# Fused block kernel: the Toeplitz matrix behind the c row and nine modulation tiles on GpSimd's DMA queue

## The chip, the cores and the metric

One core of one Trainium2 chip runs the kernel. The metric is the time of one execution in microseconds (us). The engines are TensorE (PE, with its weight loads as PEld), VectorE (DVE), ScalarE (ACT), GpSimd (POOL) and SyncE (SP). SP, ACT and POOL issue DMAs: SP on queue q1, ACT on q10, POOL on q0. Data moves between HBM, SBUF (the on-chip memory that the engines read) and PSUM (where TensorE writes, as `bank0` to `bank7`).

## The reference

One layer in float32, for 256 tokens of width 1024, cut to what matters here:

```
mod = silu(c) @ w_ada + b_ada                    # six rows of 1024: sh1 sc1 ga1 sh2 sc2 ga2
h   = rms_norm(x) * g_mix * (1 + sc1) + sh1      # and the same for 256 context tokens
proj = h @ w_in                                  # -> u_a (512), z_b (2 x 512), gate logits (2 x 1024)
y   = u_a * d + forward and backward S5 state-space scans over u_a, started from the context's state
y_a = gelu(y) * sigmoid(gelu(y) @ w_glu + b_glu)
y_b = gated spatial mixing of z_b (128-token chunks)
x   = x + ga1 * ((g_a * (y_a @ w_proj_a) + g_b * (y_b @ w_proj_b)) @ w_out)
h2  = rms_norm(x) * g_ffn * (1 + sc2) + sh2
x   = x + ga2 * (silu(gate) * val) @ w_down      # gate, val = 3x3 depthwise conv of h2 @ w_up
out = rms_norm(x) * g_final
```

## The kernel before

Everything runs once, in an order written out by hand for each engine; the engines meet through semaphores. A semaphore that a DMA raises goes up by 16.

**The weights** come in units of 1 MB (128 partitions x 2048 float32). SP loads 21 units into a ring of four slots (L312 to L334): unit u is issued when unit u - 4 has been multiplied (`s_unit`). Units 8 to 15 are the gate weights (`gate_unit(0)` to `gate_unit(7)`, L566), unit 16 is the GLU weight, 17 to 20 the projection weights. So the end of gate 1 releases unit 13 (gate 5), the end of gate 2 unit 14 (gate 6), the end of gate 3 unit 15 (gate 7), the end of gate 4 unit 16. Four units of `w_out` go to their own place (`s_wo`), and six units of `w_up` are issued at L335 to L337, once all 24 modulation sums are done (`s_mt_used` is MT = 24).

**The S5 branch.** The inputs of the scans are computed by chunks of 8 tokens (`chunk_inputs`, L553). A Toeplitz matrix holds what the tokens of a chunk do to each other. It is computed by TensorE, copied by ACT and stored to `k_scratch` in HBM (`s_k_out`), and read back from there by eight DMAs of POOL, shifted by one lag each, into `m_toep` (L371 to L374, 256 KB each in rows of 512 bytes; `s_m`). TensorE multiplies with it at L629 to L637, after gate 5; then come gate 6, the product with the scan's carries (L641 to L651), gate 7, eight transposes (L656 to L660) and three projections of y_b. DVE adds the skip term u * d (L1430 to L1435, called the skip below), ACT applies gelu (L920), TensorE the GLU product (L684 to L693), ACT the sigmoid, DVE the product y_a (L1440 to L1442), TensorE the remaining projections (L697 to L704). For each of the eight output tiles DVE merges the two branches (L1449 to L1457). The out stage (L706 to L731 on TensorE) multiplies with `w_out` by seven Strassen products, for which DVE forms sums (L1463 to L1476).

**The modulation rows** ga1, sh2 and sc2 are not matrix products: for each of MT = 24 tiles of 128 outputs, POOL loads a tile of w_ada (512 KB, `mod_tile`), and DVE multiplies it with the row silu(c) and sums over it (`modulation_sums`, L1415 to L1422). The row c is loaded by POOL (`c_bc`, L377, 512 KB) and put through silu by ACT (L905). MTS = 9 buffers hold the tiles; seven of them and `c_bc` lie where the scan's input weights were, which are free when the last chunk input is in PSUM (`s_e_ps` is 8), and the last two where the gating parameters were (`s_sgu_ps` is 2). Tile t >= 9 is issued when sum t - 9 is done. The first eight sums give ga1 (L1426), the other sixteen sh2 and sc2 (L1479). POOL's queue goes on with the reload of x (L385), the row ga1 (L389) and the row g_final (L391).

**Order on POOL**: gating parameters, eight Toeplitz DMAs, wait for all of them to land, c row, 24 tiles, x, ga1, g_final.
**Order on DVE from the scan on**: scan, y_b, sums 0 to 11, ga1, skip, sums 12 to 17, y_a, sums 18 and 19, then one sum behind each of the first four merges, the sums for the out stage, the modulation result (L1479), the updates of x.

Of the kernel before, what the change touches and what calls it, by code (L numbers as in the profile page):

```python
# [30 lines left out]
G, H, N = 32, 16, 64  # L31
# [3 lines left out]
T = 8  # L35
# [18 lines left out]
MT = 3 * KD  # L54
MTS = 9
# [24 lines left out]
def build(nc, x_t, x_tok, ctx_t, pk, s5raw, early_w, ring_w, out_w, up_w, ln, sgu_w, sgu_b, mod_w, c_row, g_row, out):  # L80
    with ExitStack() as ctx:
# [3 lines left out]
        def sem(name):  # L85
            return ctx.enter_context(nc.semaphore(name))
# [12 lines left out]
        m_toep = m_region.rearrange("p (g m) -> p g m", g=G)  # L99
# [101 lines left out]
        def par(name):  # L201
            a, b = _PK[name]
            return pk_sb[:, a:b]
# [9 lines left out]
        k_dram = nc.dram_tensor("k_scratch", [KS, P, LAGS * H], F32)  # L213
# [31 lines left out]
        s_k_ps, s_k, s_k_out, s_m = sem("k_in_psum"), sem("k_evacuated"), sem("k_stored"), sem("m_loaded")  # L245
# [29 lines left out]
        s_mt_used = sem("mod_tile_summed")  # L275
# [76 lines left out]
        @block.gpsimd  # L352
        def _(pool):
            pool.memset(ones[:, :], 1.0).then_inc(s_const, 1)
            pool.memset(c_pad, 0.0).then_inc(s_cpad, 1)
            pool.memset(ident[:, :], 0.0).then_inc(s_pool, 1)
            pool.wait_ge(s_pool, 1)
            pool.affine_select(out=ident[:, :], in_=ident[:, :], compare_op=ALU.not_equal, fill=1.0, base=0,
                               pattern=[[-1, P]], channel_multiplier=1).then_inc(s_const, 1)
            pool.wait_ge(s_ctx, 16)  # L360
            for k in CTX_SQUARES[2]:
                pool.tensor_tensor(h_all[:, k, 0:TOK], ctx_sb[:, k, :], ctx_sb[:, k, :], ALU.mult).then_inc(s_sqc[2], 1)
            pool.wait_ge(s_ada_ps, 2)
            pool.wait_ge(s_wsrc, 1)
            pool.memset(b_pad, 0.0).then_inc(s_pad, 1)
            pool.wait_ge(s_unit, U_V)
            pool.dma_start(sgu_b_sb[0:64, :, :], sgu_b[0:1].partition_broadcast(64)).then_inc(s_ln, 16)
            pool.dma_start(sgu_b_sb[64:128, :, :], sgu_b[1:2].partition_broadcast(64)).then_inc(s_ln, 16)
            pool.dma_start(ln_sb, ln.partition_broadcast(P)).then_inc(s_ln, 16)
            pool.dma_start(sgu_w_sb, sgu_w).then_inc(s_ln, 16)  # L370
            pool.wait_ge(s_k_out, 16)  # L371
            for tau in range(T):
                pool.dma_start(m_toep[tau * H:(tau + 1) * H, :, :],  # L373
                               k_dram[:, :, (T - 1 - tau) * H:(2 * T - 1 - tau) * H].rearrange("m (g h) n -> h (m g) n", h=H)).then_inc(s_m, 16)  # L374
            pool.wait_ge(s_e_ps, 8)
            pool.wait_ge(s_m, 16 * T)
            pool.dma_start(c_bc, c_row.partition_broadcast(P)).then_inc(s_crow, 16)  # L377
            for t in range(MT):
                if t == S5_TILES:
                    pool.wait_ge(s_sgu_ps, 2)  # L380
                if t >= MTS:
                    pool.wait_ge(s_mt_used, t - MTS + 1)
                pool.dma_start(mod_tile[t % MTS], mod_w[t].rearrange("p (k n) -> p k n", k=4)).then_inc(s_mt[t % MTS], 16)  # L383
            pool.wait_ge(s_y8_ps, 2)
            pool.dma_start(x1_tok.rearrange("p h f n -> p (h f n)"), x_tok).then_inc(s_xr, 16)  # L385
            pool.wait_ge(s_ga1_out, 16)
            pool.wait_ge(s_ya, KS)
            pool.wait_ge(s_unit, U_GLU + 1)
            pool.dma_start(ga1_bc.rearrange("p f n -> p (f n)"), ga1_dram[:].partition_broadcast(P)).then_inc(s_ga1_row, 16)  # L389
            pool.wait_ge(s_unit, U_PROJ + 3)  # L390
            pool.dma_start(g_bc.rearrange("p f n -> p (f n)"), g_row.partition_broadcast(P)).then_inc(s_grow, 16)  # L391
            pool.sem_inc(s_act, 2)
            with pool.Fori(0, KF // 2) as i:
                for b in range(2):
                    pool.wait_ge(s_silu, i * 2 + (b + 1))
                    pool.tensor_tensor(ffn_act[:, bass.ds(i * 2 + b, 1), :].rearrange("p a t -> p (a t)"), silu_sb[:, b, :],  # L396
                                       conv[:, b, TOK:2 * TOK], ALU.mult).then_inc(s_act, 1)
# [641 lines left out]
        def _(dve):  # L1039
# [7 lines left out]
            def settle():  # L1047

                dve.wait_ge(s_dve, count[0])

            def tt(o, a, b, op):
                mark(dve.tensor_tensor(o, a, b, op))  # L1052
# [298 lines left out]
            for j in range(1, BLK):  # L1351
                h = blocks[:, j - 1]
# [51 lines left out]
            for j in range(4):  # L1404
# [3 lines left out]
                t = merge_tmp[:, j % 2, :]  # L1408
# [6 lines left out]
            def modulation_sums(t0, t1):  # L1415

                for t in range(t0, t1):
                    dve.wait_ge(s_mt[t % MTS], 16 * (t // MTS + 1))
                    if t == 0:
                        dve.wait_ge(s_cbc, 1)  # L1420
                    dve.scalar_tensor_tensor(out=mod_tile[t % MTS], in0=mod_tile[t % MTS], scalar=1.0, in1=c_bc4, op0=ALU.mult, op1=ALU.mult,  # L1421
                                             accum_out=mod_sum[:, t:t + 1]).then_inc(s_mt_used, 1)  # L1422

            modulation_sums(0, 12)
            dve.wait_ge(s_mt_used, 12)
            dve.tensor_tensor(mod2[:, 0:KD], mod_sum[:, 0:KD], par("b_ada")[:, 2 * KD:3 * KD], ALU.add).then_inc(s_ga1, 1)  # L1426

# [6 lines left out]
                                             scalar=par("s5_d")[:, m:m + 1], in1=y_ps[:, m], op0=ALU.mult, op1=ALU.add).then_inc(s_y, 1)  # L1435

            modulation_sums(12, 18)

            for m in range(KS):  # L1440
                dve.wait_ge(s_glu, m + 1)
                dve.tensor_tensor(y_a[:, m, :], y_gelu[:, m, :], glu_gate[:, m, :], ALU.mult).then_inc(s_ya, 1)  # L1442

            modulation_sums(18, 20)

            wo11, wo12, wo21, wo22 = w_out[:, :, 0, 0, :], w_out[:, :, 0, 1, :], w_out[:, :, 1, 0, :], w_out[:, :, 1, 1, :]
# [1 line left out]
            for m in range(KD):  # L1449
                dve.wait_ge(*((s_unit, U_PROJ + m // 2 + 1) if m % 2 else (s_pr_ps, m // 2 + 1)))  # L1450
                src = bank[PROJ_BANK[m % 4]]
                t = merge_tmp[:, 0, :], merge_tmp[:, 1, :]
                tt(t[0], src[:, 0:TOK], gates[:, m, :], ALU.mult)
                tt(t[1], src[:, TOK:2 * TOK], gates[:, KD + m, :], ALU.mult)
                settle()
                dve.tensor_tensor(merged[:, m, :], t[0], t[1], ALU.add).then_inc(s_mg, 1)
                dve.wait_ge(s_mg, m + 1)  # L1457
                if m < MT - 20:
                    modulation_sums(20 + m, 21 + m)
                elif m == 6:  # L1460
                    for i in range(KD // 2):
                        dve.wait_ge(s_wo[i], 16)
                    dve.tensor_tensor(out_t1, wo12, wo11, ALU.subtract).then_inc(s_to, 1)  # L1463
# [10 lines left out]
            dve.tensor_tensor(out_s[2], m12, out_s[1], ALU.subtract).then_inc(s_so, 1)  # L1474
            dve.tensor_tensor(m21, m11, m21, ALU.subtract).then_inc(s_so, 1)
            dve.tensor_tensor(wo12, wo22, wo12, ALU.subtract).then_inc(s_to, 1)  # L1476

            dve.wait_ge(s_mt_used, MT)
            dve.tensor_tensor(mod2[:, KD:MT], mod_sum[:, KD:MT], par("b_ada")[:, 3 * KD:5 * KD], ALU.add).then_inc(s_mod2, 1)  # L1479
# [293 lines left out]
```

## Time and profile before

| | |
|---|---|
| three runs | 465.65, 466.66, 468.84 us; median 466.66 |
| the profiled execution | 465.06 us, of which the span is 463.2 |
| DMA | 98.47 MB, mean 213 GB/s |
| queue q1 (SP) | 72.34 MB, 44.8% of 16 engines' span |
| queue q0 (POOL) | 18.61 MB, 12.9% |
| TensorE's mean granted clock | 0.999 |

The span is what lies between the first and the last instruction of the profiled execution. Busy time says how full an engine was, not what it held up: an engine that is idle while another one has work costs nothing. A bracket behind a row of a timeline gives the idle time in front of it, and what ended it. DMA shares are of the 16 DMA engines' time.

### The profile page before, as it was taken

The page shows a single profiled execution, that of the slowest core. Times are in us where ns is not written, and L with a number is a line of the kernel's source. Part 1 is how long each engine was busy: PE and PEld are TensorE (multiplying, and loading weights), DVE is VectorE, ACT ScalarE, POOL GpSimd, SP SyncE. Part 2 cuts the span into 40 slices and gives each one's busy share as a digit, 9 for nine tenths or more (in the row PEclk, how much of TensorE's full clock was granted, in tenths as well). Part 3 has the DMA queues.
Part 4 walks back from the last instruction along what each step waited for, and adds up shares of the span by engine and source line. Part 5 has one row for each costly group of instructions (what it writes and reads, how often), then busy time and mean ns, then how long its engine had stood idle before and what let it go on. Part 6 is the DMA issues. An engine that isn't in the chain of part 4 may idle for free.

```text
span 463.2 us, 7678 instructions
## 1 busy us (share of the span) xinstructions
PE 447.6 (97%) x2637; PEld 345.0 (74%) x2637; DVE 401.2 (87%) x818; ACT 116.5 (25%) x216; POOL 45.3 (10%) x73
## 2 busy tenths in 40 slices
PE   8999999989999998999999999999999999999994
PEld 5677857888888886785478888888888887444453
DVE  3599999999999867969836999999999999899744
ACT  5423355135104023201152222122122122200002
POOL 2001100002104222000000111011011011000000
PEclk9999999999999999999999999999999999999999
DMA  8994499943999999989069554554554354400002
GB/s 300 418 420 162 130 347 87 299 161 72 109 219 411 419 392 399 416 342 398 3 253 405 206 190 148 209 226 162 200 201 150 147 181 70 158 0 0 1 0 91
DMA packets 24604, 98.47 MB, mean 213 GB/s; under 512 B 7608, under 2 KB 9280, under 8 KB 16128
## 3 DMA queue, kind: packets, MB, share of 16 engines
q1 hardware_dynamic: 14592, 72.34, 44.8%
q0 software_dynamic: 5056, 18.61, 12.9%
q10 hardware_dynamic: 4928, 7.14, 4.2%
q8 instruction: 18, 0.29, 0.3%
q14 instruction: 10, 0.08, 0.1%
HBM read 95.49 MB, written 2.60 MB: 212 GB/s over the span
## 4 chain that ended last, share of the span: by engine, by line
PE 59%; DVE 20%; DMA 16%; POOL 2%; ACT 1%; issue 1%; DVEq 0%; SPq 0%; ACTq 0%; POOLq 0%
PE bank L756 33%; PE bank L767 14%; DVE s_region L1052 11%; DMA h_all<-mod_w 9%; PE bank L711 5%; DMA s_region<-k_scratch 5%; PE bank L667 5%; DVE s_region L1171 2%; DMA ctx_region<-ctx_t 2%; DVE s_region L1309 1%; DVE h_all L1225 1%; POOL s_region L373 1%; PE bank L482 1%; POOL s_region L383 1%; DMA k_scratch<-s_region 1%
## 5 line engine op out<-in xcount | busy, mean ns | idle before, releaser
L756 PE MATMUL bank<-h_all,s_region 128*128 128x256 f32 x704 | 152.3, 379 | 0.2 <-ACT h_all L966 0.2
L756 PEld LDWEIGHTS bank<-h_all,s_region 128*128 128x128 f32 x704 | 133.2, 190 | 19.1 <-ACT h_all L966 0.6
L1571 DVE SCALAR_TENSOR_TENSOR ctx_region<-ctx_region,pk_sb 128x189 f32<-128x189 f32 (+2 forms) x352 | 130.2, 443 | 0.3 <-DVE ctx_region L1571 0.2
L573 PE MATMUL bank<-h_all,ring_region 128*128 128x256 f32 x256 | 56.2, 380 | 0.3 <-DVE s_region L1340 0.3
L573 PEld LDWEIGHTS bank<-h_all,ring_region 128*128 128x128 f32 x256 | 48.4, 190 | 7.4 <-DVE s_region L1340 0.5
L767 PE MATMUL bank<-s_region,ring_region 128*128 128x512 f32 (+1 forms) x132 | 47.8, 522 | 0.0
L767 PEld LDWEIGHTS bank<-s_region,ring_region 128*128 128x128 f32 x132 | 25.0, 190 | 22.5 <-issue 20.3
L984 ACT ACTIVATE ctx_region<-bank 128x512 f32<-128x512 f32 x22 | 13.1, 597 | 113.3 <-PE bank L756 60.1
L1052 DVE TENSOR_TENSOR s_region<-s_region,power 128x2048 f32<-128x2048 f32 (+1 forms) x16 | 38.1, 2420 | 0.2
L396 POOL TENSOR_TENSOR ring_region<-gates,ctx_region 128x256 f32 x22 | 17.2, 784 | 178.2 <-ACT gates L992 178.2
L482 PE MATMUL bank<-h_all,ring_region 128*128 128x256 f32 x128 | 31.1, 388 | 0.2 <-ACT h_all L829 0.2
L1421 DVE SCALAR_TENSOR_TENSOR s_region<-s_region 128x1024 f32<-128x1024 f32 x20 | 24.1, 1223 | 7.8 <-DMA s_region<-mod_w 7.6
L667 PE MATMUL bank<-z_region,ring_region 128*128 128x256 f32 x128 | 28.2, 380 | 1.1 <-DVE z_region L1442 1.1
L482 PEld LDWEIGHTS bank<-h_all,ring_region 128*128 128x128 f32 x128 | 23.3, 190 | 5.9 <-ACT h_all L829 2.5
L667 PEld LDWEIGHTS bank<-z_region,ring_region 128*128 128x128 f32 x128 | 24.2, 190 | 4.7 <-DVE z_region L1442 1.5
L1560 DVE TENSOR_SCALAR ctx_region<-ctx_region,pk_sb 128x256 f32<-128x256 f32 x22 | 11.5, 521 | 11.6 <-ACT ctx_region L984 10.9
L871 ACT ACTIVATE gates<-bank,pk_sb 128x256 f32<-128x256 f32 x16 | 6.7, 470 | 39.6 <-PE bank L573 39.6
L533 PE MATMUL bank<-ring_region,h_all 128*128 128x512 f32 x32 | 16.4, 593 | 0.0
L1017 ACT ACTIVATE z_region<-s_region 128x512 f32<-128x512 f32 (+1 forms) x4 | 2.3, 573 | 50.3 <-DVE s_region L1637 31.6
L829 ACT ACTIVATE h_all<-h_all,mod,scale 128x256 f32<-128x256 f32 x16 | 8.8, 594 | 23.7 <-DVE scale L1233 21.6
L521 PEld LDWEIGHTS bank<-ident,s_region 128*128 128x128 f32 x64 | 7.9, 141 | 8.8 <-issue 7.9
L711 PE MATMUL bank<-s_region,h_all 128*128 128x512 f32 (+1 forms) x40 | 14.2, 507 | 0.0
(242 smaller groups left out, 529.5 us busy)
## 6 DMA issues: line engine op xcount, KB each, us to landing
s_region<-up_w SPq DMA_DIRECT2D x33, 1024.0 KB, 4.9
ring_region<-ring_w SPq DMA_DIRECT2D x20, 1024.0 KB, 9.0
s_region<-mod_w POOLq DMA_DIRECT2D x20, 512.0 KB, 15.4
s_region<-early_w SPq DMA_DIRECT2D x4, 1024.0 KB, 21.8
s_region<-out_w SPq DMA_DIRECT2D x4, 1024.0 KB, 12.7
gates<-mod_w ACTq DMA_DIRECT2D x8, 512.0 KB, 5.4
gates<-early_w SPq DMA_DIRECT2D x2, 1024.0 KB, 10.8
s_region<-k_scratch POOLq DMA_DIRECT2D x8, 256.0 KB, 12.4
```

Of the source, the lines that this page charges most:

```text
L396: pool.tensor_tensor(ffn_act[:, bass.ds(i * 2 + b, 1), :].rearrange("p a t -> p (a t)"), silu_sb[:, b, :], conv[:, b, TOK:2 * TOK], ALU.mu ...
L482: mx = pe.matmul(bank[m][:, cols], ring[:, U_INU + k // 4, ((k % 4) * KS + m) * P:((k % 4) * KS + m + 1) * P], h_all[:, k, cols], start=(k ...
L533: mx = pe.matmul(bank[6 + c][:, :], h_x[:, k, c * P:(c + 1) * P], ring[:, u % RING, kk * 512:(kk + 1) * 512], start=(k == 0), stop=(k == K ...
L573: mx = pe.matmul(bank[5 - j % 2][:, mm * TOK:(mm + 1) * TOK], ring[:, u % RING, (mm * KD + k) * P:(mm * KD + k + 1) * P], h_x[:, k, :], st ...
L667: mx = pe.matmul(bank[PROJ_BANK[m % 4]][:, (1 - half) * TOK:(2 - half) * TOK], ring[:, u % RING, t * P:(t + 1) * P], src[:, k, :], start=( ...
L711: mx = pe.matmul(bank[OUT_BANK[n]][:, cols], lhs(i), rhs(i)[:, cols], start=(i == 0 and n not in (3, 6, 7)), stop=(i == KD // 2 - 1), skip ...
L756: mx = pe.matmul(bank[s % 3][:, half * TOK:(half + 1) * TOK], up_ring[:, s, (half * KD + k) * P:(half * KD + k + 1) * P], h2[:, k, :], sta ...
L767: mx = pe.matmul(bank[PRODUCT_BANK[n]][:, cols], lhs(i), rhs(i)[:, cols], start=(i == 0), stop=(i == PAIRS_D - 1))
L984: act.activation(up_sb[:, j % 2, :], bank[(j % USLOTS) % 3][:, :], ACT.Copy).then_inc(s_upsb, 1)
L1052: mark(dve.tensor_tensor(o, a, b, op))
L1421: dve.scalar_tensor_tensor(out=mod_tile[t % MTS], in0=mod_tile[t % MTS], scalar=1.0, in1=c_bc4, op0=ALU.mult, op1=ALU.mult, accum_out=mod_ ...
L1571: dve.scalar_tensor_tensor(out=o, in0=a, scalar=cw[:, tile[half], (dy + 1) * 3 + dx + 1], in1=o, op0=ALU.mult, op1=ALU.add).then_inc(s_con ...
```

## The change

On POOL the wait for the last chunk input, the c row and the first nine tiles (0 to 8) now stand ahead of the Toeplitz matrix, whose eight DMAs are issued when the loop reaches t = MTS = 9; the wait for their landing on POOL is gone (TensorE's own wait at L629 stays). On DVE nine sums, not twelve, stand ahead of the skip, five between the skip and y_a (9 to 13), three behind y_a (14 to 16), one behind each of the first six merges (17 to 22), and the last one (23) behind the sums of the out stage. The number of DMAs, sums and matmuls stays the same.

```diff
-            pool.wait_ge(s_k_out, 16)
-            for tau in range(T):
-                pool.dma_start(m_toep[tau * H:(tau + 1) * H, :, :],
-                               k_dram[:, :, (T - 1 - tau) * H:(2 * T - 1 - tau) * H].rearrange("m (g h) n -> h (m g) n", h=H)).then_inc(s_m, 16)
             pool.wait_ge(s_e_ps, 8)
-            pool.wait_ge(s_m, 16 * T)
             pool.dma_start(c_bc, c_row.partition_broadcast(P)).then_inc(s_crow, 16)
             for t in range(MT):
                 if t == S5_TILES:
                     pool.wait_ge(s_sgu_ps, 2)
+                if t == MTS:
+                    pool.wait_ge(s_k_out, 16)
+                    for tau in range(T):
+                        pool.dma_start(m_toep[tau * H:(tau + 1) * H, :, :],
+                                       k_dram[:, :, (T - 1 - tau) * H:(2 * T - 1 - tau) * H].rearrange("m (g h) n -> h (m g) n", h=H)).then_inc(s_m, 16)
                 if t >= MTS:
                     pool.wait_ge(s_mt_used, t - MTS + 1)
...
-            modulation_sums(0, 12)
-            dve.wait_ge(s_mt_used, 12)
+            modulation_sums(0, 9)
+            dve.wait_ge(s_mt_used, 9)
...
-            modulation_sums(12, 18)
+            modulation_sums(9, 14)
...
-            modulation_sums(18, 20)
+            modulation_sums(14, 17)
...
-                if m < MT - 20:
-                    modulation_sums(20 + m, 21 + m)
+                if m < 6:
+                    modulation_sums(17 + m, 18 + m)
...
             dve.tensor_tensor(wo12, wo22, wo12, ALU.subtract).then_inc(s_to, 1)
+            modulation_sums(23, MT)
```

## Rows read from the trace of the kernel before

**Rows 1.** The page, part 1: busy us, share of the span, instructions.
```profile
PE 447.6 (97%) x2637; PEld 345.0 (74%) x2637; DVE 401.2 (87%) x818; ACT 116.5 (25%) x216; POOL 45.3 (10%) x73
```

**Rows 2.** Timeline of PE: start us, us, engine, line, operation, count [idle before it <-what ended it].
```profile
108.25 2.08 PE L562 MATMUL bank<-ctx_region,s_region 128*64 128x64 f32 x64
...
147.07 1.95 PE L635 MATMUL bank<-s_region,ctx_region 128*32 128x128 f32 x64
...
170.93 1.04 PE L658 MATMUL bank<-ident,ctx_region 128*128 128x128 f32 x8
...
176.98 0.27 PE L682 MATMUL bank<-ident,mod 128*8 128x128 f32 x1
179.51 7.14 PE L688 MATMUL bank<-u_x,ring_region 128*128 128x256 f32 x32 [2.26 <-ACT u_x L920]
186.49 1.89 PE L667 MATMUL bank<-z_region,ring_region 128*128 128x256 f32 x8
189.47 20.99 PE L667 MATMUL bank<-z_region,ring_region 128*128 128x256 f32 x96 [1.09 <-DVE z_region L1442]
...
238.50 21.71 PE L756 MATMUL bank<-h_all,s_region 128*128 128x256 f32 x99 [0.15 <-ACT h_all L966]
```

**Rows 3.** Timeline of DVE.
```profile
155.28 1.22 DVE L1421 SCALAR_TENSOR_TENSOR s_region<-s_region 128x1024 f32<-128x1024 f32 x1
...
175.10 2.15 DVE L1434 SCALAR_TENSOR_TENSOR ctx_region<-u_x,pk_sb,bank 128x128 f32<-128x128 f32 x8
...
187.99 1.43 DVE L1442 TENSOR_TENSOR z_region<-u_x,ctx_region 128x256 f32<-128x256 f32 x4
...
207.12 0.76 DVE L1052 TENSOR_TENSOR merge_tmp<-bank,gates 128x256 f32<-128x256 f32 x2 [2.24 <-PE bank L667]
...
221.53 0.69 DVE L1052 TENSOR_TENSOR gates<-ctx_region,u_x 128x512 f32<-128x512 f32 x1 [1.60 <-ACT ctx_region L936]
```

**Rows 4.** Timeline of ACT: gelu, and the last two sigmoids of the GLU.
```profile
177.29 2.08 ACT L920 ACTIVATE u_x<-ctx_region 128x1024 f32<-128x1024 f32 x1 [3.81 <-DVE ctx_region L1434]
...
186.69 0.84 ACT L929 ACTIVATE ctx_region<-bank,pk_sb 128x256 f32<-128x256 f32 x2 [2.62 <-PE bank L688]
```

**Rows 5.** Timeline of POOL: the issues.
```profile
112.73 5.01 POOL L373 DMA_DIRECT2D s_region<-k_scratch  x8 [54.19 <-DMA k_scratch<-s_region]
...
139.26 3.69 POOL L383 DMA_DIRECT2D s_region<-mod_w  x7
142.91 1.53 POOL L383 DMA_DIRECT2D h_all<-mod_w  x2
```

**Rows 6.** Issues of L373 to landing: least, median, most.
```profile
DMA to landing us min/median/max: 5.5/12.4/21.0
```

**Rows 7.** Windows: us, busy of PE, PEld, DVE, ACT, POOL; clock, DMA share, GB/s.
```profile
120.00:125.00 5.00, 5.00 (x25) 4.41 (x24) 4.86 (x8) 0.39 (x2) 0.00 (x0) 1.00 1.04 108
...
150.00:155.00 5.00, 5.00 (x25) 4.41 (x24) 4.80 (x13) 0.00 (x0) 0.00 (x0) 1.00 1.03 420
```

**Rows 8.** DMA queues, 112.7 to 138.1 us: packets, MB, share of 16 engines.
```profile
q0 software_dynamic: 640, 2.10, 68.5%
q1 hardware_dynamic: 212, 1.61, 28.6%
```

**Rows 9.** DMA, 119.4 to 126.4 us: the only data queue, and the issue of unit 13.
```profile
q0 software_dynamic: 232, 0.76, 104.4%
...
ring_region<-ring_w SPq DMA_DIRECT2D x1, 1024.0 KB, 18.2
```

**Rows 10.** Timelines of PE, at the kernel's start and mid-kernel: the same filler matmuls.
```profile
1.00 5.12 PE L408 MATMUL bank<-ones 128*128 128x256 f32 x14 [1.00 <-POOL ones L354]
...
236.01 1.46 PE L408 MATMUL bank<-ones 128*128 128x256 f32 x6
```

**Rows 11.** The six first issues of up weights on SP, and the page's median landing.
```profile
201.58 3.19 SPq L337 DMA_DIRECT2D s_region<-up_w  x6
...
s_region<-up_w SPq DMA_DIRECT2D x33, 1024.0 KB, 4.9
```

## The prediction

> **What bounds the kernel now.** I read the page's shares first, then TensorE's timeline between 108 and 240 us, then the waits of DVE and ACT at each place where TensorE stood, and last the DMA queues. TensorE is busy for 97% of the span [rows 1], so a change that leaves its work alone can only give back its waits. In the stretch that the change touches there are two: 2.26 us before the GLU product, ended by ACT's gelu, and 1.09 us before the projections of y_a, ended by DVE [rows 2]. Behind both stands DVE's order. The skip starts at 175.10 [rows 3] though TensorE's transposes were done at 170.93 + 1.04 = 171.97 [rows 2]; DVE was still at sums, which waited for tiles. And y_a starts at 187.99 [rows 3] though its last sigmoids end at 186.69 + 0.84 = 187.53 [rows 4], because DVE sat in a sum. The third thing to see is a margin: the Toeplitz product starts at 147.07 without a wait [rows 2], and the last of the eight matrix DMAs lands at 117.1 + 21.0 = 138.1 [rows 5, 6]. That is 9.0 us of slack, and it is what the change spends.
>
> **What it gives back.** Sums 0 to 8 need only tiles that now come early. DVE starts them at 155.28 as before [rows 3]; nine at 1.15 us each (start to start) end by 165.7. The skip then starts when the transposes allow, about 171.6, and lasts 2.15: done by 173.9. Gelu (2.08) ends by about 176.1, ahead of TensorE, which is free for the GLU at 176.98 + 0.27 = 177.25. The wait of 2.26 is gone. Sums 9 to 13 follow the skip, 5 x 1.15 = 5.8 us, done by 179.7; the first sigmoid is not due before half the GLU, 177.25 + 3.6 = 180.8. So y_a can follow each sigmoid; the last is done 0.4 us after the sigmoids' end, inside the projection that TensorE has left (its 1.89 us reach to 0.85 us past them [rows 2, 4]). The 1.09 is gone as well. Gain: **3.35 us**. Nothing else follows on TensorE: it is next late for nothing in this part.
>
> **What the other sums cost: nothing, under these covers.** Behind y_a stand three sums where there were two, +1.15; with no wait ahead of them the merges start about 0.8 us later against TensorE than before. Merges 4 and 5 get a sum each, 2.3 us, against DVE's 2.24 us idle before merge 6 and about 1 us before merge 5 (the former in [rows 3]). Merge 6 comes out on time. Without this cover up to 1 us would go to the out stage. Sum 23 (1.2 us) stands before DVE's 1.60 us wait for ACT's copy [rows 3]; 0.4 us remains, and at worst 1.2 is lost. The six up weights wait for sum 23, so SP issues them not at 201.58 [rows 11] but some 20 us later, near 221 in the old clock. A unit lands in 4.9 us in the median [rows 11] on idle queues, and the first is needed at 238.50 [rows 2]: 10 us to spare. POOL's x, ga1 and g_final move behind tile 23, whose issue now waits for y_a; that is some 4 us for x and nothing for ga1, which waited for y_a already. DVE asks for x and ga1 at 221.5.
>
> **What the matrix costs.** Each term is a shift of 138.1, the old landing.
> - POOL starts on its queue when the last chunk input is done, 108.25 + 2.08 = 110.33 [rows 2], not when the matrix is stored, 112.73 [rows 5]: -2.4.
> - Ahead of the matrix go ten transfers of 512 KB, 5.24 MB. Such data flows at about 0.41 MB per us when the queues are full (420 GB/s in 150 to 155 [rows 7]): +12.7. POOL's issues (ten in about 5.8 us [rows 5]) end near 116.1, long before; its issue speed doesn't decide.
> - Unit 13, issued at 119.4, now falls among the tiles instead of into the matrix: 1.05 MB, +2.5. Gate 5 needs it at 140, so it is in time.
> - That gives 151.0 with as much of SP's traffic beside the matrix as before. In the old run SP's packets held back while the matrix ran: unit 13 was issued at 119.4, and until 126.4 only q0 moved data; it landed 18.2 us after its issue [rows 9]. Between 112.7 and 138.1 q1 got 1.61 MB, 28.6% of the engines' time, and the matrix 68.5% [rows 8]. In the new run unit 14 is issued (126.4) just as the matrix starts (about 127), 15 at 133.3 and 16 at 140.3. All three are there earlier relative to the matrix, so I count one more unit: +2.5.
>
> Landing **153.5**, wait of TensorE 153.5 - 147.1 = **6.4 us**. The bounds: at best no SP packet gets beside the matrix, 151.0 less 28.6% of 25.4 us = 143.8, no wait. At worst units 14 to 16 alternate with it in full: 3.15 MB at 7.3/1.61 us per MB is 14.3 us, against the 7.3 already counted: 158, a wait of 11. I take 6.4 since it is nearest to how rows 8 and 9 split the time. The matrix is costly for its size: 108 GB/s with the engines fully busy, against 420 [rows 7].
>
> A page makes a rule of the sharing. The Trainium skill, "DMA: Bandwidth & Descriptors", section on queues, rings and completion order, says that each DMA engine takes turns between its queues packet by packet. By that rule unit 14 would alternate from its issue, and the landing would be at the upper end, near 158. Rows 9 speak against it for the first 7 us after an issue, and rows 8 for it after that.
>
> Everything behind the Toeplitz product on TensorE moves by the wait. DVE's sums 0 to 8 don't, and the carries are ready by 155, so no second wait is added; the 3.35 stays a gain. **Sum: 6.4 - 3.35 = +3.1 us.** Against the profiled 465.06 that is 468.2; that execution lies 1.6 below the median of the three runs, 466.66, to which I add the same: **469.8 us**.
>
> **The rivals.**
> 1. *The matrix comes in time* (faster). Place: the Toeplitz product. If SP's units keep behind the matrix as unit 13 did in rows 9, it lands by 147.1 and only the gain is left: 466.66 - 3.35 = 463.3. It decides at a landing of 150.4: below that the kernel is faster. For it: rows 9. Against it: the second half of rows 8.
> 2. *The wait also costs TensorE its clock* (slower still). At the start, after an idle stretch, fourteen filler matmuls took 5.12 us; six took 1.46 mid-kernel [rows 10]. At the latter pace fourteen take 3.2, so a start from rest costs 1.9. The longest wait inside the touched stretch is 2.26 us, at a granted clock of 1.00. A wait of 6 us is outside what the trace shows. Time: 469.8 + 1.9 = 471.7. The Trainium skill, "TensorE: Matmul & The Clock Gate", warns that an idle gap in the middle of a kernel puts the array back to 1.2 GHz; by it this rival is the rule whenever the wait comes. No row here shows such a gap.
> 3. *Gate 5 waits instead.* If unit 13 is held behind tiles and matrix together, it lands near 147 instead of 128, gate 5 stands some 7 us from 140, and the Toeplitz product no longer waits: 466.66 + 7 - 3.35 = 470.3. Against it: unit 16, issued at 140.3 among tiles, did not suffer so.
> 4. *The two cancel*: landing near 150.4, no difference. The order on DVE then works and shows nothing.
>
> **How the numbers follow.** Forecast 0.40; rival 2, 0.27; rival 1, 0.15; rival 4, 0.10; rival 3, 0.08. About 1%, 4.7 us, is what a measurement can tell from no change. The gain is capped at 3.35, so faster by over 1% needs something unseen: 0.04. Slower by over 1% needs a wait of 8 us, or 6.1 with the clock's cost: a fifth of the forecast, most of rival 2, half of rival 3, together 0.34. The rest, 0.62, is within 1%. The range leaves out the lower edge of rival 1 and the last tenth above: 464.0 to 475.0.
>
> **What would show it.** In TensorE's timeline: a DMA wait in front of L635 (forecast 6.4 us; none in rival 1), or in front of gate 5 (rival 3). No wait on gelu before L688, none on DVE before the last L667 group. In the queues: the first tiles at about 112, the matrix between 127 and 153 at a little over 100 GB/s. Gate 6 behind the wait at a granted clock below 1.00 would be rival 2. What would make me wrong: a matrix that moves faster once no other issue interrupts it, or DMA engines that serve q0 strictly first.

## The result: 13 us slower, and the profile after

The changed kernel takes 479.65 us in the median of five runs (479.14 to 484.71); the kernel before 466.66 (465.65 to 468.84, five runs). The ratio is 1.031, with an interval of 1.028 to 1.035. The forecast was 469.8 in a range of 464.0 to 475.0: the direction was right, the size was a quarter of the real one. The profiled execution took 481.89 us, 16.8 more than that of before, at a mean granted clock of 0.972. The first row below is the page's part 1, the second the granted clock in 40 equal slices of the span.

```profile
PE 453.3 (94%) x2637; PEld 350.0 (73%) x2637; DVE 400.2 (83%) x818; ACT 116.6 (24%) x216; POOL 45.2 (9%) x73
...
PEclk9999999999997597999999999999999999999998
```

TensorE's share fell from 97% to 94% for the same 2637 matmuls, and the clock, which was at 9 in all forty slices before, has two dips, at 144 to 168 us and at 180 to 192 (the 8 in the last slice lies behind the last matmul). TensorE's timeline shows where; compare [rows 2].

```profile
161.08 3.64 PE L635 MATMUL bank<-s_region,ctx_region 128*32 128x128 f32 x64 [13.84 <-DMA s_region<-k_scratch]
164.65 8.07 PE L573 MATMUL bank<-h_all,ring_region 128*128 128x256 f32 x32
172.65 3.95 PE L648 MATMUL bank<-s_region,x_region 64*32 64x128 f32 x147
177.63 3.84 PE L648 MATMUL bank<-s_region,x_region 64*32 64x128 f32 x109 [1.04 <-issue]
181.40 9.91 PE L573 MATMUL bank<-h_all,ring_region 128*128 128x256 f32 x32
...
197.31 7.07 PE L688 MATMUL bank<-u_x,ring_region 128*128 128x256 f32 x32
204.22 22.61 PE L667 MATMUL bank<-z_region,ring_region 128*128 128x256 f32 x104
...
254.86 7.47 PE L756 MATMUL bank<-h_all,s_region 128*128 128x256 f32 x33 [0.15 <-ACT h_all L966]
```

The Toeplitz product waits 13.84 us for the matrix, where it had not waited. The GLU (L688) and the projections of y_a (joined to the ones before them, L667 x104) come without the brackets of 2.26 and 1.09 us. The first up product starts at 254.86 against 238.50: +16.4 of the 16.8. The parts, counted from start to start: the Toeplitz product starts 14.0 later, of which 13.8 are the wait; 1.7 because it takes 3.64 us and not 1.95; 0.9 for gate 6 (8.07 against 7.17); 0.9 in the second part of the carry product and the gap before it; 2.7 for gate 7 (9.91 against 7.17); less 3.9 between the transposes and the first up product (254.86 - 191.15 = 63.7, against 238.50 - 170.93 = 67.6). Of these 3.9 the two brackets make 3.35. The windows show the clock that goes with the long ones (columns as in [rows 7]).

```profile
150.00:155.00 5.00, 0.00 (x0) 0.00 (x0) 4.79 (x13) 0.00 (x0) 0.00 (x0) 0.50 1.01 215
155.00:160.00 5.00, 0.00 (x0) 0.00 (x0) 4.97 (x10) 0.00 (x0) 1.64 (x3) 0.50 0.99 298
160.00:165.00 5.00, 3.92 (x65) 3.57 (x66) 5.00 (x9) 0.00 (x0) 2.40 (x5) 0.50 0.94 338
...
180.00:185.00 5.00, 5.00 (x41) 3.87 (x31) 0.00 (x0) 1.08 (x2) 0.00 (x0) 0.51 0.02 7
```

0.50 is the lower level, 1.2 GHz. The clock fell while TensorE stood at the wait. At 180 it fell again; there TensorE had not waited for data, but it had just come through small matmuls with a gap of 1.04 us in them.

POOL's issues, and their landing (compare [rows 5, 6]):

```profile
110.46 0.55 POOL L372 DMA_DIRECT2D s_region<-c_row  x1 [51.86 <-PE bank L562]
...
116.15 5.01 POOL L379 DMA_DIRECT2D s_region<-k_scratch  x8
```
```profile
DMA to landing us min/median/max: 17.9/28.5/40.4
```

The last matrix DMA is issued at 120.5 and lands 40.4 us later, at 160.9. The DMA queues tell why. First from 128.5 to 132 us, then from 132 to 158 (columns as in [rows 8]):

```profile
q0 software_dynamic: 174, 0.59, 109.9%
```
```profile
q1 hardware_dynamic: 546, 4.06, 73.8%
q0 software_dynamic: 515, 1.66, 27.4%
```

DVE started the skip as soon as the transposes were done, and its last sum fitted in front of ACT's copy with 0.34 us left (forecast 0.4):

```profile
191.86 2.15 DVE L1434 SCALAR_TENSOR_TENSOR ctx_region<-u_x,pk_sb,bank 128x128 f32<-128x128 f32 x8 [26.10 <-PE bank L658]
...
237.90 0.69 DVE L1052 TENSOR_TENSOR gates<-ctx_region,u_x 128x512 f32<-128x512 f32 x1 [0.34 <-ACT ctx_region L936]
```

### The profile page after: what moved, and what is told of

Read it like the earlier page. It is cut to its first block, busy times and chain, and to the rows that moved or that the text cites. A ratio compares the mean times of both kernels' runs of the same rounds, so it can differ in the third digit from the quotient of the medians.

```text
span 479.9 us, 7677 instructions
## 1 busy us (share of the span) xinstructions
PE 453.3 (94%) x2637; PEld 350.0 (73%) x2637; DVE 400.2 (83%) x818; ACT 116.6 (24%) x216; POOL 45.2 (9%) x73
## 4 chain that ended last, share of the span: by engine, by line
PE 80%; DMA 14%; POOL 2%; issue 1%; SPq 1%; DVE 1%; ACT 0%; DVEq 0%; ACTq 0%
PE bank L756 32%; PE bank L767 12%; DMA s_region<-k_scratch 8%; PE bank L667 6%; PE bank L573 5%; PE bank L482 5%; PE bank L711 5%; DMA s_region<-early_w 4%; PE bank L548 3%; PE bank L533 3%; PE bank L562 2%; DMA s_region<-up_w 2%; PE bank L648 2%; PE bank L521 2%; PE bank L688 1%; PE bank L448 1%
## 5 line engine op out<-in xcount | busy, mean ns | idle before, releaser
L573 PE MATMUL bank<-h_all,ring_region 128*128 128x256 f32 x256 | 59.8, 397 | 0.5 <-DVE s_region L1340 0.5
L573 PEld LDWEIGHTS bank<-h_all,ring_region 128*128 128x128 f32 x256 | 51.0, 201 | 9.0 <-DVE s_region L1340 0.8
L482 PE MATMUL bank<-h_all,ring_region 128*128 128x256 f32 x128 | 31.1, 388 | 0.0
L667 PE MATMUL bank<-z_region,ring_region 128*128 128x256 f32 x128 | 28.0, 379 | 0.0
L482 PEld LDWEIGHTS bank<-h_all,ring_region 128*128 128x128 f32 x128 | 23.3, 190 | 5.7 <-ACT h_all L829 2.3
L667 PEld LDWEIGHTS bank<-z_region,ring_region 128*128 128x128 f32 x128 | 24.2, 190 | 3.3
L1434 DVE SCALAR_TENSOR_TENSOR ctx_region<-u_x,pk_sb,bank 128x128 f32<-128x128 f32 x8 | 2.2, 343 | 26.1 <-PE bank L658 26.1
L383 POOL DMA_DIRECT2D s_region<-mod_w x20 | 10.6, 533 | 77.0 <-DVE s_region L1421 77.0
L635 PE MATMUL bank<-s_region,ctx_region 128*32 128x128 f32 x64 | 3.6, 420 | 13.8 <-DMA s_region<-k_scratch 13.8
L533 PE MATMUL bank<-ring_region,h_all 128*128 128x512 f32 x32 | 16.4, 593 | 0.0
```

The costliest lines, as they stand in the source:

```text
L482: mx = pe.matmul(bank[m][:, cols], ring[:, U_INU + k // 4, ((k % 4) * KS + m) * P:((k % 4) * KS + m + 1) * P], h_all[:, k, cols], start=(k ...
L533: mx = pe.matmul(bank[6 + c][:, :], h_x[:, k, c * P:(c + 1) * P], ring[:, u % RING, kk * 512:(kk + 1) * 512], start=(k == 0), stop=(k == K ...
L573: mx = pe.matmul(bank[5 - j % 2][:, mm * TOK:(mm + 1) * TOK], ring[:, u % RING, (mm * KD + k) * P:(mm * KD + k + 1) * P], h_x[:, k, :], st ...
L667: mx = pe.matmul(bank[PROJ_BANK[m % 4]][:, (1 - half) * TOK:(2 - half) * TOK], ring[:, u % RING, t * P:(t + 1) * P], src[:, k, :], start=( ...
```

## The experiments

Theory: the landing of the matrix sets the time, and it is late because SP's ring units alternate with it packet by packet; the rest of the loss is TensorE's clock; the order on DVE is a gain of its own. Rivals: bytes ahead and the matrix's own slowness; costs of the order on DVE; another cause of the long matmuls. Ratios are to the kernel before on the same chip.

### The two halves of the change

**Only the order on DVE.** POOL's part of the diff taken back.

> The queue order of POOL is that of the kernel before (matrix first, wait for its landing, then c row and tiles); only DVE's order of the sums is that of the changed kernel. Theory (the matrix behind the tiles costs everything, the order of the sums gives 3.35 us): no DMA wait before the Toeplitz product, no gelu wait before the GLU product, none before the projections of y_a; about 463.3 us against 466.7, a ratio of 0.993. Rival (the new order of the sums costs something too, in the merges or the out stage): 466 or more.

461.98 us (ten runs, 461.58 to 465.61), ratio 0.994, interval 0.990 to 0.997. TensorE's timeline:

```profile
147.30 1.96 PE L635 MATMUL bank<-s_region,ctx_region 128*32 128x128 f32 x64
...
177.10 7.07 PE L688 MATMUL bank<-u_x,ring_region 128*128 128x256 f32 x32
184.01 22.61 PE L667 MATMUL bank<-z_region,ring_region 128*128 128x256 f32 x104
...
234.65 27.54 PE L756 MATMUL bank<-h_all,s_region 128*128 128x256 f32 x126 [0.15 <-ACT h_all L966]
```

No bracket is left before L688 and L667. From the Toeplitz product to the first up product it takes 87.4 us, against 91.4 [rows 2]: 4.1 less, the 3.35 of the two waits and small overlaps. Of it 3.9 lie behind the transposes, as in the changed kernel. The gain is real and does not need the early tiles.

**Only the order on POOL.** DVE's part taken back.

> POOL's queue order is that of the changed kernel, DVE's order of the sums that of the kernel before. Theory: the same wait of about 14 us before the Toeplitz product and the same clock losses behind it, and since DVE has the wait to catch up in, the gelu wait is gone as well: 478 to 481 us, a ratio of 1.025 to 1.032. Rival (a good part of the loss comes from the order on DVE): below 474.

479.44 us, ratio 1.032 (1.026 to 1.038). There is no wait before the GLU, and one of 14.91 us before the Toeplitz product:

```profile
162.00 3.64 PE L635 MATMUL bank<-s_region,ctx_region 128*32 128x128 f32 x64 [14.91 <-DMA s_region<-k_scratch]
165.57 7.47 PE L573 MATMUL bank<-h_all,ring_region 128*128 128x256 f32 x32
...
180.81 7.17 PE L573 MATMUL bank<-h_all,ring_region 128*128 128x256 f32 x32
```

In this execution the clock fell at the wait alone; gate 7 took its 7.17 us. All of the loss is on POOL's queue, and there the sums' order no longer matters, since DVE catches up during the wait.

### What makes the matrix late

**SP holds the ring from unit 14 on.**

```diff
-            with sp.Fori(2, full) as i: ...
+            for u in range(2 * RING, UNITS):
+                sp.wait_ge(s_unit, u - RING + 1)
+                if u == 14:
+                    sp.wait_ge(s_m, 16 * T)
                 ...
```

> The changed kernel, but SP does not issue unit 14 (gate 6) and those behind it until the matrix has landed (SP's loop is written out; nothing else differs). Theory of the alternation (from about 132 us on every packet of the matrix waits for an 8 KB packet of the ring, units 14 to 17): alone the matrix needs some 18 to 20 us, so it lands near 147 to 149 instead of 160.9; unit 14 then lands 5 us later, and gate 6 stands for it until 152 to 154. Both waits together 4 to 6 us, less the 3.35: 467 to 470 us. Rival (the matrix is late because of the 5 MB ahead and its own slowness, whatever the ring does): it lands at 157 or later, and 478 or more.

The timeline of TensorE, the landing of the matrix, and q0 from 130 to 144 us, where no other data queue moved:

```profile
147.30 1.95 PE L632 MATMUL bank<-s_region,ctx_region 128*32 128x128 f32 x64
151.88 8.86 PE L570 MATMUL bank<-h_all,ring_region 128*128 128x256 f32 x32 [2.63 <-DMA ring_region<-ring_w]
```
```profile
DMA to landing us min/median/max: 17.8/22.7/26.7
```
```profile
q0 software_dynamic: 543, 1.77, 102.9%
```

The same tiles are ahead, and the matrix lands at 120.4 + 26.7 = 147.1: TensorE does not wait for it. Alone it moved 39 records (0.126 MB) per us, next to the ring 20 (0.064 MB). The rival is refuted: 13.8 of the 13.8 us between the two landings are the four units. The time was still 473.8 us (ratio 1.020, 1.014 to 1.027), more than the 467 to 470 that I had expected: gate 6 stood 2.63 us for unit 14, and in that execution the clock fell behind that wait and again in the carry product (gate 6 took 8.86 us, gate 7 9.42).

**SP holds the ring from unit 16 on.** The same edit with `u == 16`.

> The changed kernel, but SP holds unit 16 and those behind it until the matrix has landed, so that units 14 and 15 alternate with it and 16 and 17 don't (all four held: landing 147.1; none held: 160.9). Theory of the alternation (each unit beside the matrix costs it the same): about half of the difference, landing 153 to 155, a wait of 6 to 8 us; 471 to 476 us, according to the clock. Rival (only the unit that is in flight at the end of the matrix counts, or only the first one): landing within 2 us of 147 or of 161.

```profile
155.83 3.64 PE L632 MATMUL bank<-s_region,ctx_region 128*32 128x128 f32 x64 [8.52 <-DMA s_region<-k_scratch]
```

476.26 us (ratio 1.020, 1.017 to 1.023), the matrix in at 155.7. Of SP's units beside it none, two and four give 147.1, 155.7 and 160.9: 4.3 us each for the first two, 2.6 each for the others, the last of which was issued only at about 147.3. Each is one profiled execution, and with all four beside it the landing varied from 160.9 to 163.2, so the split is rough.

**The matrix late, with no tile near it.** POOL as before, DVE as changed, and

```diff
             pool.wait_ge(s_k_out, 16)
+            pool.wait_ge(s_unit, U_GATE + 3)
```

> The version with only DVE's order changed, but POOL waits with the matrix until gate 2 is done (126.4 us); c row and tiles stay behind its landing, so no tile is near it. Theory (the tiles matter only because they move the matrix beside units 14 to 17): data from 127.7, packets of the ring beside it from about 131, landing 159 to 162, a wait of 12 to 14 us, as in the changed kernel; 476 to 483 us. Rival (the tiles slow the matrix themselves, for example since they have filled its queue): it lands like the matrix of the kernel before, 25 us after its issue, at 152 to 154.

Issued from 126.88 on, the last landed 26.3 us after its issue at 131.3: 157.6, a wait of 10.72 us, one run of 474.22 (expected 476 to 483). That lies between theory and rival, nearer to the theory. Unit 14 had been issued half a microsecond earlier and passed first (5.5 us to its landing); from 132 to 142 only the matrix moved, though unit 15 had been issued at 133.3; the alternation came after that. So the tiles are not needed for a late matrix, but in the changed kernel they filled most of the start that it otherwise has to itself: some 3 us of it, 129 to 132, were left to the matrix.

**The ring held while the matrix is first.** The order of before with DVE's new one, SP holding from unit 13 on.

> The version with only DVE's order changed, but SP holds unit 13 and those behind it until the matrix has landed. Theory: alone the matrix needs 18 to 19 us from its first data at 114: landing 132.5 to 133.5 instead of 138; unit 13 lands near 138.5, gate 5 needs it at 140.3, so nothing waits, 461 to 464 us. Rival (the ring does not slow the matrix when it comes first, since only q0 moved data until 129): landing 137 to 138 all the same, and gate 5 stands 2 us or more.

One run, 461.69. POOL's next issue, released by the landing, moved from 138.71 to 134.66:

```profile
134.66 0.57 POOL L374 DMA_DIRECT2D s_region<-c_row  x1 [17.48 <-DMA s_region<-k_scratch]
```

Of the 4.05 us, 0.54 are the matrix's earlier issue (112.19 against 112.73). So 1.61 MB of the ring had cost the old matrix some 3.5 us, not the 7.3 that its share of the engines' time comes to (28.6% of 25.4 us [rows 8]). The landing, at about 134.0, came 0.5 to 1.5 us later than expected; TensorE waited for no DMA.

**Four tiles ahead instead of nine.** `if t == MTS` becomes `if t == 4`.

> The changed kernel with four tiles ahead of the matrix instead of nine (2.6 MB instead of 5.2). Theory of the alternation (the matrix moves about 35 records per us until SP's packets show up, and 19 after that): it starts at 118, gets 8 us for itself, and needs 20 us for the rest beside units 13 to 15: landing 148 to 149.5, a wait of 1 to 2.5 us; 463 to 466 us. Rival (a plain shift by the bytes ahead, 5 x 1.27 us less than with nine tiles, counted from the measured 160.9): landing 154.5, a wait of 7, 470 us or more with the clock.

```profile
152.67 3.64 PE L635 MATMUL bank<-s_region,ctx_region 128*32 128x128 f32 x64 [5.63 <-DMA s_region<-k_scratch]
```

469.27 us (ratio 1.004, 1.002 to 1.007), landing 152.6: neither my 148 to 149.5 nor the rival's 154.5. The matrix started at 120, not at 118, and had some 8.5 us to itself; the alternation from 129 on went at 19 records per us as reckoned. It shows that nine was not an unlucky number: four tiles already cost more than the order on DVE gives.

**The matrix first, without the wait for its landing.** The better version that the first results pointed to: L376's wait removed, the rest as in the first experiment.

> POOL issues the matrix first, as before, but no longer waits for its landing: c row and nine tiles are issued right behind it; DVE's order of the sums is the changed one. Theory (the old wait for the landing only kept the tiles back, and on one queue they come behind the matrix anyway): the matrix lands near 138 to 139 as before, no wait before the Toeplitz product, the tiles land by about 160 instead of 170; nothing on TensorE depends on that, so the time is that of the version with only DVE's order changed, 461 to 463 us. Rival (tile packets already on the queue slow the matrix or the ring): a DMA wait before a gate or the Toeplitz product, 465 or more.

463.67 us (twelve runs, 462.44 to 467.08), ratio 0.995 (0.993 to 0.998). No DMA wait on TensorE. The time is a little above the 461 to 463 expected, with an interval that overlaps that of the first experiment. The old wait on POOL cost nothing, and its removal gives nothing.

### What the clock costs

A filler is a matmul of ones into a free bank, which only keeps TensorE busy.

**Sixty fillers in the wait.**

```diff
+            filler(3, 60)
             pe.wait_ge(s_m, 16 * T)
```

> The changed kernel with sixty filler matmuls (of ones, into a free bank) on TensorE ahead of its wait for the matrix: 60 x 0.216 = 13 us of work that fits into the 13.8 us of waiting. Theory (the clock is lost because TensorE stands, and costs 2.6 us in the Toeplitz product and gate 6, and in some executions another 3 us around gate 7): granted clock 1.00 through the Toeplitz product, which takes 2.0 us instead of 3.6, gate 6 7.2 instead of 8.1; 475 to 477 us. Rival (these stretches are long for another reason, as DMA traffic beside them): no change, 479.6. If the second fall of the clock near 180 us has the first as its cause, it is gone as well, and the time is 473.5 to 475.

I had the price wrong: a filler is two instructions, 0.434 us, and sixty take 26 us. 486.3 us (ratio 1.046, 1.040 to 1.051). The timeline behind them:

```profile
146.95 26.06 PE L408 MATMUL bank<-ones 128*128 128x256 f32 x120
172.94 1.95 PE L636 MATMUL bank<-s_region,ctx_region 128*32 128x128 f32 x64
174.83 7.17 PE L573 MATMUL bank<-h_all,ring_region 128*128 128x256 f32 x32
181.93 7.07 PE L649 MATMUL bank<-s_region,x_region 64*32 64x128 f32 x256
188.93 7.17 PE L573 MATMUL bank<-h_all,ring_region 128*128 128x256 f32 x32
```

With the clock at 1.00 all through, the Toeplitz product is back at 1.95 us and both gates at 7.17.

**Thirty fillers.**

> As the version with sixty fillers, which took 26 us and not 13 (each is two instructions, 0.434 us): thirty, 13.0 us, inside the wait of 14. Theory: granted clock 1.00 all through; Toeplitz product 1.95 us, gate 6 7.17, gate 7 7.17; time 479.6 less 2.6 us for the first fall of the clock and up to 4 us for the second: 473.5 to 477. Rival (fillers next to the DMA wait delay the matrix, or the clock falls again in the carry product all the same): 478 or more.

479.43 us (ratio 1.028, 1.025 to 1.030), not the 473.5 to 477 expected: no change. The matrix came only at 163.2 in the profiled execution, 3.00 us of standing remained, and the clock fell (0.50 from 165 to 167 us):

```profile
147.14 13.11 PE L408 MATMUL bank<-ones 128*128 128x256 f32 x60
163.25 2.92 PE L636 MATMUL bank<-s_region,ctx_region 128*32 128x128 f32 x64 [3.00 <-DMA s_region<-k_scratch]
```

**Thirty-six fillers.**

> The changed kernel with thirty-six fillers (15.6 us) ahead of the wait for the matrix, to reach 162.8 us, where it has landed in four runs out of five (160.9, 162.0, 162.3, 163.2 seen). Theory: no or next to no wait is left, the granted clock stays at 1.00 and, as in the version with sixty, the part from the Toeplitz product to the end of gate 7 takes 23.2 us instead of 26.9 to 30.2: 475 to 476.5 us, all runs close together. Rival (the clock falls in the carry product in any case): 479 and a clock below 0.99.

```profile
162.84 1.96 PE L636 MATMUL bank<-s_region,ctx_region 128*32 128x128 f32 x64 [0.32 <-DMA s_region<-k_scratch]
164.72 7.17 PE L573 MATMUL bank<-h_all,ring_region 128*128 128x256 f32 x32
171.82 5.47 PE L649 MATMUL bank<-s_region,x_region 64*32 64x128 f32 x203
179.17 2.94 PE L649 MATMUL bank<-s_region,x_region 64*32 64x128 f32 x53 [1.87 <-issue]
182.04 9.27 PE L573 MATMUL bank<-h_all,ring_region 128*128 128x256 f32 x32
```

The first fall is bridged (1.96 and 7.17 us), yet the time is 481.02 (ratio 1.034, 1.029 to 1.038): the clock fell in the carry product, whose gap and gate 7 took 1.87 and 9.27 us. ("Issue" in a bracket means that the profile shows nothing that TensorE waited for.) The second fall does not need the first. My expectation of 475 to 476.5 failed.

**Two fillers between the halves of the carry product**, in the version with only DVE's order changed.

```diff
                 mx.then_inc(s_y8_ps, 1)
+                if g2 == 0:
+                    filler(3, 2)
```

> The version with only DVE's order changed, with two fillers (0.9 us) between the two halves of the product with the scan's carries. Some of that version's runs took 465.5 us at a mean clock of 0.989 instead of 461.6 at 0.998. Theory (the clock sometimes falls in the carry product, whose matmuls are small, and the slower runs are those): with fillers in it all runs lie within 1 us, near 462.5, at a clock of 0.996 or more. Rival (the fall has nothing to do with this product): the same two groups, 0.9 us later.

461.61 us, nine runs from 461.45 to 462.45, all at a clock of 0.996 to 0.998; ratio 0.993 (0.991 to 0.995). Without them two of ten runs had shown 0.989 and 0.990 and taken 465.6 and 465.4. The fillers cost 0.9 us of work and the median did not rise: they also fill a gap that the product has. That none of nine executions was slow, where two of ten had been, is too few to show that the fillers did it. It is the lowest median of all, but not apart from that of the version without fillers.

**The same two in the changed kernel, with and without the thirty-six.**

> The changed kernel with thirty-six fillers ahead of its wait and two between the halves of the carry product. Theory (of the changed kernel's loss what is not waiting is the clock, which falls once in the wait and once, on its own, in the carry product): granted clock 1.00 all through, 23.2 to 23.6 us from the Toeplitz product to the end of gate 7 in place of 28.5 with thirty-six fillers alone; 475 to 476.5 us in all runs. Rival (the carry product's gap and the long gate 7 have another cause than the clock): 480 to 481 as without the two fillers.

> The changed kernel with only the two fillers in the carry product. Theory: the first fall of the clock stays (Toeplitz product 3.6 us, gate 6 7.5 to 8.1), the second is gone (gate 7 7.17); 477 to 479 us, and the runs closer together than the changed kernel's 479.1 to 484.7. Rival (the second fall follows from the first): the same spread and 479.6 or more.

480.97 us (ratio 1.032, 1.027 to 1.037) and 479.87 us (1.032, 1.029 to 1.035). With both kinds the profiled execution had a gap of 0.95 us in the second half and fell all the same (gate 7 9.51 us); with the two alone it did not (7.17 us). Two fillers are no sure cure here, and neither the expected 475 to 476.5 nor the 477 to 479 was reached. What the clock costs can still be read from the profiled executions, as span less the start of the Toeplitz product, and of that the two parts in which the clock fell:

| clock behind the wait | all, us | Toeplitz product and gate 6 | carry product with its gap, and gate 7 |
|---|---|---|---|
| 1.00 all through (sixty fillers) | 484.1 - 172.9 = 311.2 | 9.0 | 14.0 |
| first fall only (POOL's order alone) | 476.8 - 162.0 = 314.8 | 11.0 | 14.9 |
| second fall only (thirty-six fillers) | 479.4 - 162.8 = 316.6 | 9.0 | 19.3 |
| both (changed kernel) | 479.9 - 161.1 = 318.8 | 11.6 | 18.5 |

So 3.6, 5.4 and 7.6 us more than with none. Not all of it is the clock: the first fall costs 2.0 to 2.6 us, the second with the gap ahead of it 4.5 to 5.3; the gap alone, without a fall, is the 0.9 in the second row, and 0.8 of that row's 3.6 lie behind gate 7. (The execution in the first row also had no gap in the carry product; the version with only DVE's order changed, at 1.00 with a gap of 0.51, gives 459.8 - 147.3 = 312.5.) The landing, on the other hand, moved between 160.9 and 163.2 from one execution to the next. That, and which fall an execution gets, can be why the medians of the versions with fillers do not come apart. Of the changed kernel's five executions, the profiled one (481.89) and that of 484.71 us had a mean clock of 0.972, the other three 0.979 to 0.984; POOL's order alone, with one fall, had 0.979. So the median of 479.65 probably has one fall. Which share each has in the medians stays open.

## Why the prediction was wrong

- **The two gains**: right. Both waits went; 3.35 us forecast, 3.9 between the transposes and the first up product, in the changed kernel and with the order on DVE alone. The new order of the sums added nothing there: POOL's order alone, with the sums as before, takes the same 63.7 us. All covers held: the merges, the last sum (0.34 us left), the late up weights.
- **The matrix** is the step that failed, by its term for SP's traffic. The shift by the queue's earlier start, the tiles and unit 13 was right: held free of the ring, the matrix landed at 147.1, where the old pattern without SP's share would give 151.0 less 3.5, the measured cost of that share in the old order (my best case took 7.3 off and was too early). But "I count one more unit: +2.5" was wrong twice: the term measured 160.9 - 151.0 = 9.9 us. There were four units, not about two and a half, since unit 17 is issued when gate 5 ends, just as TensorE begins to stand. And a unit beside the matrix costs it 2.6 to 4.3 us. The landing was 160.9, not 153.5, and even my worst case, 158, left unit 17 out.
- **The reading of rows 9** was the root. I took "only q0 moved data" for a rule of this traffic. It was a delay at the start: nearly 10 us before the ring's first packet in the old kernel (119.4 to 129) and with the matrix late and alone (133.3 to 143), 9 with four tiles ahead (119.4 to 128.5), 5.6 in the changed kernel (126.4 to 132). What sets it was not found. After it the queues take turns to the end. The page that I argued against had it right: the Trainium skill, "DMA: Bandwidth & Descriptors", on queues, rings and completion order, has every engine go round its queues packet by packet, and the trace agrees from 132 us on, with 546 records of q1 and 515 of q0.
- **Rival 1**, in time by 147: what would have come true had SP been silent (the held ring shows it). **Rival 3**, gate 5 waiting: no, unit 13 landed 8.5 us after its issue. **Rival 4**: no.
- **Rival 2**, the clock, came true and I had priced it at 1.9 us with a chance of 0.27. It cost 2.6 in the Toeplitz product and gate 6, and then 3.6 from the carry product to gate 7, 0.3 of them a longer gap, which was on no list of mine. The warning of "TensorE: Matmul & The Clock Gate" in the Trainium skill, that an idle gap brings 1.2 GHz, agrees with the 0.50 in the windows. It belonged into the forecast: at a wait of 5.63 us, shorter than the 6.4 that I forecast, the Toeplitz product took 3.64 us (four tiles ahead).

With the wait at 13.8 and the clock at 2.0 (one fall) to 6.2 (both, with the longer gap), less 3.9, the sum is 11.9 to 16.1; measured were 13.0 in the medians and 16.8 in the profiled pair, where the Toeplitz product also had 0.2 more of delay ahead of the wait and 0.3 to 0.4 came behind the first up product.

## What to carry to other kernels

Slack in front of a transfer is not spent at the rate of the bytes put ahead of it: ask also which transfers of other queues it will then run beside, to its end, and count those that the stalled engine's own progress releases. What it loses goes by records, not by bytes: it gave way one record for each of its own, and the other queue's were twice as large. The matrix came down from 0.126 MB per us to 0.064 that way. The tiles in 4 KB records lost as well, from 0.41 (118 to 123 us) to 0.13 beside unit 13 (124 to 127 us). And a wait on TensorE of a few microseconds is not over when the data is there; give it a second term for the clock.

## What the hardware showed that I had not expected

- The matrix with its 512 byte rows, alone: 39 records per us with the ring held, 30 to 34 in the kernel before, with four tiles ahead, with the matrix first and the ring held, and with the matrix late; why they differ was not found. Beside the ring: 20. The pair of an 8 KB packet and a matrix record then takes the 16 engines some 0.8 us of each one's time, so the ring slows as well: unit 14 to 16 landed after 15.3 to 15.8 us, on idle queues 4.8 (unit 13 with the matrix late).
- The granted clock fell once each behind standing of 2.63 us (ring held, after the 1.95 us of the Toeplitz product) and 3.00 us (thirty fillers); behind the 2.26 us of the kernel before it stayed at 1.00.
- It also fell without such a wait, in the carry product: 256 matmuls of 128 columns in about 7 us, with a gap named "issue" inside. In the profiled executions with a fall there the gap was 0.95 to 2.08 us; in those without one, 0 to 1.00. So the size of the gap does not decide alone, and whether it brings the fall was not shown.
- The gap goes with a transfer of instructions. In all thirteen profiled executions that have it, a record of 16 KB on queue q8 ("instruction") ends 1.25 to 1.49 us before the gap does; in the changed kernel it starts at 175.3 and ends at 176.4, and TensorE goes on at 177.63. That fits a sequencer that has run out of instructions in a row of matmuls of 28 ns. No run was made to test it.
